# A gather queue on GpSimd: every second gather of one table waits for the landing of that table's gather before last

## The chip, the core and the metric

The kernel runs on one core of a Trainium2 chip. The metric is the time of one execution in microseconds on the device. A run is timed without the profiler; one further execution is profiled and gives the trace. Engines: TensorE (PE; its weight loads are PEld), VectorE (DVE), ScalarE (ACT), GpSimd (POOL), and SyncE (SP), which here issues the loads of the weights. Transfers are done by 16 DMA engines, whichever engine issues them.

## The reference, cut to what matters

Two transformer blocks run one after the other over 256 tokens of width 1024 in float32. The first ends in a product-key expert layer, which is the stage of the change:

```
idx = 16 experts of 16384 for each of 8 heads          # 128 experts for each token
u   = take(u_tab, idx)                                  # [tokens, 128, 1024]
a   = einsum('chkd,cd->chk', u, x)                      # a dot product for each token and expert
wgt = g * gelu(a)
v   = take(v_tab, idx)
out = einsum('chk,chkd->cd', wgt, v)                    # weighted sum of 128 rows for each token
```

Ahead of it are the modulation, attention and a short convolution; behind it the whole second block (a state space mixer, a linear attention in chunks, a feed-forward of width 4096).

## The kernel before, in words

The 256 tokens are two tiles of 128 tokens, one token on each partition. Each tile has 128 experts, so the stage has 256 steps, e = 0 to 255, here called experts (EXPERTS = 128 for a tile). For each e one row of each table is fetched for each of the 128 tokens:

- **u(e)**, the gather of the first table (`peer_u`, line 687): 128 rows of 4 KB into one of NU = 5 buffers of the tensor `gathered`. Its landing raises the semaphore `u_full[e % 5]` by 16.
- **v(e)**, the gather of the second table (`peer_v`, line 701): as many bytes into one of NV = 7 buffers. Its landing raises `v_full[e % 7]` by 16.

GpSimd issues both kinds from one program, in the order u(0), v(0), u(1), u(2), v(1), u(3), v(2), u(4), v(3) and so on: v(e) stands behind u(e+1). It has nothing else to do in the stage. Since an engine works off its program in order, a wait ahead of one gather holds all gathers behind it. All gathers go through one queue of transfers.

The consumers follow the landings. VectorE multiplies u(e) with the tile's tokens and adds up (`dot_expert`, line 2489), then raises `dot_ready` by 1. ScalarE takes the dot through the gelu, multiplies it with the gate and writes it on a diagonal, `diag[e % 8]` (lines 1737 to 1746). TensorE multiplies this diagonal with v(e) in two matmuls of 512 columns (`sum_expert`, line 1143; the trace shows two records for each matmul and each weight load, four for an expert) and accumulates in PSUM; after every odd e it raises `pair_summed` by 1. Between the experts TensorE does other products, by tables such as WQ_AT, and VectorE the routing of later heads; SyncE loads weights of 2 MB each when a buffer for them comes free.

What keeps a gather from overwriting rows in use are waits on GpSimd: u(e) waits for `dot_ready` to reach e - 4, and v(e) for `pair_summed` to reach `pairs(e - 6)`, which is (e - 5) // 2. The sum of expert e - 7, whose buffer v(e) takes, is then done.

Of the kernel before, what the change touches and what calls it, by code (L numbers as in the profile page):

```python
# [70 lines left out]
NV = 7  # L71
# [173 lines left out]
def pairs(experts):  # L245

    return (experts + 1) // 2


def build(nc, T, out):  # L250

    with ExitStack() as ctx:
# [3 lines left out]
        def sem(name):  # L256
            return ctx.enter_context(nc.semaphore(name))
# [187 lines left out]
        v_full = [sem(f"v_full{i}") for i in range(NV)]  # L445
        S_ = {}

        def flag(name):

            if name not in S_:  # L450
                S_[name] = sem(name)
            return S_[name]

        def group_wait(eng, name, i):
            g = (name, i)
            eng.wait_ge(bank_full[GROUP_BANK[g]], GROUP_USE[g] + 1)
# [52 lines left out]
        def turn_wait(eng, *u):  # L509

            eng.wait_ge(turned, turn_no[u] + 1)
# [124 lines left out]
        def _(pool):  # L636
# [55 lines left out]
            def gather_v(e):  # L692

                r, k, slot = e // ROUTE, e % ROUTE, e % NV
                if e >= NV:
                    pool.wait_ge(flag("pair_summed"), pairs(e - NV + 1))
                if e == 0:
                    turn_wait(pool, "m", 1, 0)
                if e == 3:
                    group_wait(pool, "out1", 1)  # L700
                pool.indirect_dma_start(  # L701
                    v_rows[:, slot, :], None, T["peer_v"],
                    bass.IndirectOffsetOnAxis(ap=expert_idx[:, r % 2, k:k + 1], axis=0),
                ).then_inc(v_full[slot], 16)

            gather_u(0)
            gather_v(0)
            gather_u(1)
            for e in range(1, TT * EXPERTS):
                if e + 1 < TT * EXPERTS:  # L710
                    gather_u(e + 1)
                gather_v(e)
# [2468 lines left out]
```

## Time and profile before

| | us |
|---|---|
| timed, median of 3 (lowest to highest) | 1310.25 (1309.9 to 1311.06) |
| span of the profiled execution | 1366.9 |
| of it ahead of the gathers | 150 |
| of it the stage of the gathers | 762 |
| of it behind them | 455 |

The profiled execution is 56.6 us longer than the median of the timed ones. Busy time is the sum of an engine's instructions. A row that ends in `<-` and a name says what ended the idle time ahead of an instruction; "issue" means that nothing which the profile shows did, "remote" that the semaphore moved but the profile can't name who moved it. The two gathers appear as DMA_INDIRECT on POOL; their duration there is that of the issue, not of the transfer.

### The profile page before, as it was taken

Reading aid. Unit: us, or ns where it says so; the run is one execution under the profiler, and the core shown is the slowest. Engines: PE = TensorE matmul, PEld = TensorE weight load, DVE = VectorE, ACT = ScalarE, POOL = GpSimd, SP = SyncE. Lnnn points to the kernel's source line nnn. Section 1 sums busy time; section 2 is a strip of 40 time slices with the busy share of each in tenths; the row PEclk is TensorE's granted clock in tenths of the full one; section 3 lists DMA queues with packets and bytes.
Section 4 is the critical chain, followed back from the end, with each engine's and each line's share of the span. In section 5 each row is a group of like instructions: output and inputs, shape, how many; then the busy total and the mean of one; then the engine's idle time right before and its main releaser. Section 6 shows DMA issues by size and latency. Waiting matters only on the chain. (4 is left out here: it accounts for less than half of the span.)

```text
span 1366.9 us, 14592 instructions
## 1 busy us (share of the span) xinstructions
PE 1199.9 (88%) x4663; PEld 665.4 (49%) x4663; DVE 861.8 (63%) x1765; ACT 420.2 (31%) x1138; POOL 500.2 (37%) x580
## 2 busy tenths in 40 slices
PE   7899888888778978876788889789999999999997
PEld 4676554433344542222345433236544545999443
DVE  2657669574663654776746557679989543676345
ACT  2213334344223343343423324432323311222000
POOL 1000356666665666766666666630000000000000
PEclk9999999999998999999999999999999999999999
DMA  9998789999998999999999999986644444454450
GB/s 358 390 349 326 286 319 339 367 357 367 364 366 300 406 403 405 407 377 364 340 371 353 400 405 409 377 306 233 224 139 148 145 150 156 157 175 145 175 184 31
DMA packets 134303, 405.66 MB, mean 297 GB/s; under 512 B 10153, under 2 KB 11585, under 8 KB 133971
## 3 DMA queue, kind: packets, MB, share of 16 engines
q0 software_dynamic: 75024, 273.19, 53.1%
q1 hardware_dynamic: 57860, 127.48, 25.8%
q10 hardware_dynamic: 1342, 4.06, 0.8%
q8 instruction: 38, 0.62, 0.2%
q14 instruction: 39, 0.31, 0.1%
HBM read 403.12 MB, written 1.05 MB: 296 GB/s over the span
## 5 line engine op out<-in xcount | busy, mean ns | idle before, releaser
L1143 PE MATMUL psum<-gathered,modr 128*128 128x512 f32 x1024 | 505.0, 633 | 130.3 <-DMA gathered<-in_peer_v_dram,expert_idx 49.0
L2489 DVE CUSTOM_DVE_ANT_0 gathered<-gathered,psum 128x1024 f32<-128x1024 f32 x256 | 311.5, 1217 | 202.3 <-DMA gathered<-in_peer_u_dram,expert_idx 153.3
L1143 PEld LDWEIGHTS psum<-gathered,modr 128*128 128x128 f32 x1024 | 190.7, 199 | 404.7 <-issue 284.9
L687 POOL DMA_INDIRECT gathered<-in_peer_u_dram,expert_idx x256 | 244.9, 957 | 240.5 <-DVE expert_idx L1997 144.0
L701 POOL DMA_INDIRECT gathered<-in_peer_v_dram,expert_idx x256 | 242.6, 947 | 169.9 <-remote 73.7
L780 PE MATMUL psum<-featT,weight_ring 128*128 128x128 f32 (+2 forms) x960 | 145.3, 305 | 14.4 <-issue 11.3
L780 PEld LDWEIGHTS psum<-featT,weight_ring 128*128 128x128 f32 x960 | 133.7, 196 | 43.9 <-issue 35.6
L780 PE MATMUL psum<-weight_ring,featT 128*128 128x512 f32 x336 | 147.9, 596 | 1.3 <-ACT featT L1563 0.8
L1737 ACT ACTIVATE gel<-dots 128x1 f32<-128x1 f32 x256 | 51.1, 200 | 255.1 <-issue 128.1
L1746 ACT ACTIVATE modr<-ident,wgt 128x128 f32<-128x128 f32 x256 | 102.8, 402 | 18.5 <-issue 1.1
L780 PEld LDWEIGHTS psum<-weight_ring,featT 128*128 128x128 f32 x336 | 62.6, 190 | 78.8 <-issue 76.6
L1741 ACT ACTIVATE wgt<-gel,expert_gate 128x1 f32<-128x1 f32 x256 | 75.4, 294 | 17.9 <-issue 0.3
L1989 DVE TENSOR_TENSOR work<-work 128x1088 f32<-128x1088 f32 (+5 forms) x87 | 68.6, 801 | 9.6 <-issue 2.8
L725 POOL DMA_DIRECT2D gathered<-in_b_in_dram x6 | 5.3, 942 | 138.6 <-ACT gathered L1585 104.2
L1585 ACT COPY work<-psum 128x128 f32<-128x128 f32 x32 | 8.4, 262 | 81.5 <-remote 44.6
L1978 ACT ACTIVATE work<-work,pack 128x256 f32<-128x256 f32 x28 | 12.7, 500 | 56.8 <-DVE work L1989 56.8
L1989 DVE TENSOR_TENSOR vectors<-weight_ring 128x1024 f32<-128x1024 f32 x14 | 16.5, 1220 | 20.9 <-PE psum L1512 20.9
L1563 ACT COPY featT<-psum 128x512 f32<-128x512 f32 (+1 forms) x24 | 12.4, 554 | 55.0 <-PE psum L752 53.8
L780 PE MATMUL psum<-weight_ring,uT 128*128 128x512 f32 x64 | 28.2, 593 | 1.0 <-ACT gathered L1585 1.0
L1989 DVE TENSOR_TENSOR gathered<-gathered,psum 128x256 f32<-128x256 f32 (+1 forms) x17 | 8.6, 511 | 29.8 <-PE psum L780 24.9
L1473 PE MATMUL psum<-featT,weight_ring 128*128 128x128 f32 x224 | 27.3, 275 | 0.0
L1473 PEld LDWEIGHTS psum<-featT,weight_ring 128*128 128x128 f32 x224 | 26.1, 192 | 0.0
(443 smaller groups left out, 1343.1 us busy)
## 6 DMA issues: line engine op xcount, KB each, us to landing
weight_ring<-in_w_in_dram SPq DMA_DIRECT2D x16, 2048.0 KB
weight_ring<-in_w_up_dram SPq DMA_DIRECT2D x8, 2048.0 KB
weight_ring<-in_w_down_dram SPq DMA_DIRECT2D x8, 2048.0 KB
weight_ring<-in_ada_w_dram SPq DMA_DIRECT2D x5, 2048.0 KB
work<-in_ada_w_dram SPq DMA_DIRECT2D x5, 2048.0 KB, 16.3
weight_ring<-in_peer_wq_dram SPq DMA_DIRECT2D x3, 2048.0 KB
gathered<-in_ada_w_dram SPq DMA_DIRECT2D x2, 2048.0 KB, 14.5
gathered<-in_peer_u_dram,expert_idx POOLq DMA_INDIRECT x256
```

The source lines that it names most:

```text
L687: pool.indirect_dma_start(u_rows[:, slot, :], None, T["peer_u"], bass.IndirectOffsetOnAxis(ap=expert_idx[:, r % 2, k:k + 1], axis=0),).the ...
L701: pool.indirect_dma_start(v_rows[:, slot, :], None, T["peer_v"], bass.IndirectOffsetOnAxis(ap=expert_idx[:, r % 2, k:k + 1], axis=0),).the ...
L780: last = pe.matmul(psum[0:m, bank, 0:n], lhs(k), rhs(k), start=(k == 0), stop=(k == kt - 1))
L1143: mm = pe.matmul(psum[:, SUM_BANK + half, :], diag[:, e % 8, :], v_rows[:, slot, 512 * half:512 * (half + 1)], start=(e % EXPERTS == 0), s ...
L1473: last = pe.matmul(psum[:, UP_BANKS * (n % 2) + bank, at:at + P], a(g, m), b(g), start=(g == 0), stop=(g == 3))
L1563: ins = act.activation(dst, src, func, **kw) if func else act.copy(dst, src)
L1737: act.activation(gel[:, col:col + 1], dots[:, col:col + 1], ACT.Gelu_apprx_tanh)
L1741: act.activation(wgt[:, col:col + 1], gel[:, col:col + 1], ACT.Copy, scale=expert_gate[:, r % 2, k:k + 1])
L1746: act.activation(diag[:, e % 8, :], ident[:, :], ACT.Copy, scale=wgt[:, col:col + 1]).then_inc(flag("diag_full"), 1)
L1978: act.activation(ffT[:, k, :], ffT[:, k, :], ACT.Relu, bias=pk("b_up")[:, k:k + 1])
L1989: return dve.tensor_tensor(o, a, b, op)
L2489: dve.tensor_tensor_reduce(u_rows[:, slot, :], u_rows[:, slot, :], h2_rows[t], 1.0, 0.0, ALU.mult, ALU.add, dots[:, col:col + 1])
```

## The change

From e = 8 on, an even v(e) no longer waits for `pair_summed`. It waits until v(e-2) has landed: for `v_full[(e - 2) % 7]` to have been raised by all gathers into that buffer up to v(e-2). Odd v(e) and all u(e) are unchanged.

```
             def gather_v(e):
 
                 r, k, slot = e // ROUTE, e % ROUTE, e % NV
-                if e >= NV:
+                if e >= NV and e % 2:
                     pool.wait_ge(flag("pair_summed"), pairs(e - NV + 1))
+                elif e >= NV:
+                    pool.wait_ge(v_full[(e - 2) % NV], 16 * ((e - 2) // NV + 1))
                 if e == 0:
                     turn_wait(pool, "m", 1, 0)
```

The order in which GpSimd's instructions stand is the same; what each waits for is not. This is GpSimd's program before, from v(8) on (v(8), u(10), v(9), u(11), v(10), u(12)); the name in brackets is the semaphore:

```order
L701 DMA gathered<-in_peer_v_dram,expert_idx 128x1024 [waits pair_summed]
L687 DMA gathered<-in_peer_u_dram,expert_idx 128x1024 [waits dot_ready]
L701 DMA gathered<-in_peer_v_dram,expert_idx 128x1024 [waits pair_summed]
L687 DMA gathered<-in_peer_u_dram,expert_idx 128x1024 [waits dot_ready]
L701 DMA gathered<-in_peer_v_dram,expert_idx 128x1024 [waits pair_summed]
L687 DMA gathered<-in_peer_u_dram,expert_idx 128x1024 [waits dot_ready]
```

And this is the same place of the changed program, where the gathers of the second table have moved to line 703:

```order
L703 DMA gathered<-in_peer_v_dram,expert_idx 128x1024 [waits v_full6]
L687 DMA gathered<-in_peer_u_dram,expert_idx 128x1024 [waits dot_ready]
L703 DMA gathered<-in_peer_v_dram,expert_idx 128x1024 [waits pair_summed]
L687 DMA gathered<-in_peer_u_dram,expert_idx 128x1024 [waits dot_ready]
L703 DMA gathered<-in_peer_v_dram,expert_idx 128x1024 [waits v_full1]
L687 DMA gathered<-in_peer_u_dram,expert_idx 128x1024 [waits dot_ready]
```

v(8) now waits for buffer 6, into which v(6) went, and v(10) for buffer 1, into which v(8) went. Three gathers stand between the one that is waited for and the one that waits.

## Rows read from the trace of the kernel before

**Rows 1.** The page: the span and the slices of it.

```profile
span 1366.9 us, 14592 instructions
...
GB/s 358 390 349 326 286 319 339 367 357 367 364 366 300 406 403 405 407 377 364 340 371 353 400 405 409 377 306 233 224 139 148 145 150 156 157 175 145 175 184 31
```

**Rows 2.** Busy time by window: the gathers' stage.

```profile
core 0: us, PE busy (x) PEld busy (x) DVE busy (x) ACT busy (x) POOL busy (x), PEclk, DMA share, GB/s
150.00:912.00 762.00, 619.97 (x1851) 298.83 (x1851) 480.80 (x1164) 283.48 (x881) 487.42 (x512) 0.95 0.97 371
```

**Rows 3.** Busy time by window: single stretches of the stage.

```profile
286.00:299.00 13.00, 10.77 (x36) 5.01 (x34) 8.09 (x16) 6.39 (x15) 9.91 (x11) 1.00 0.99 389
205.00:240.00 35.00, 29.01 (x96) 15.04 (x95) 31.04 (x92) 14.17 (x42) 23.78 (x25) 0.90 0.95 339
349.00:361.00 12.00, 8.13 (x28) 3.75 (x27) 8.56 (x29) 2.73 (x10) 8.75 (x10) 1.00 0.90 307
820.00:860.00 40.00, 36.65 (x83) 14.98 (x82) 28.86 (x69) 18.17 (x52) 27.11 (x29) 1.00 1.03 410
```

**Rows 4.** Busy time by window: the stage cut in five.

```profile
155.00:205.00 50.00, 43.28 (x149) 22.96 (x148) 32.92 (x98) 18.13 (x51) 29.87 (x32) 0.93 0.92 334
205.00:440.00 235.00, 190.93 (x617) 97.71 (x616) 146.97 (x361) 87.12 (x275) 150.59 (x159) 0.93 0.95 351
440.00:540.00 100.00, 82.70 (x287) 42.04 (x285) 55.07 (x129) 35.71 (x115) 64.27 (x67) 0.97 1.03 404
540.00:760.00 220.00, 173.96 (x455) 78.84 (x456) 144.85 (x355) 80.11 (x256) 143.70 (x152) 0.93 0.97 371
760.00:912.00 152.00, 124.10 (x314) 53.12 (x313) 97.07 (x202) 61.13 (x183) 96.83 (x102) 0.99 1.02 399
```

**Rows 5.** GpSimd in order of time: start, duration, engine, line, idle before.

```profile
349.51 0.94 POOL L701 DMA_INDIRECT gathered<-in_peer_v_dram,expert_idx  x1 [3.56 <-remote]
350.75 0.94 POOL L687 DMA_INDIRECT gathered<-in_peer_u_dram,expert_idx  x1 [0.30 <-issue]
```

**Rows 6.** GpSimd's waits in 150 to 912 us: total, times, longest.

```profile
POOL gathered L701 <- remote: 73.7, 29, 4.2
...
POOL gathered L701 <- PE psum L1143: 28.7, 12, 8.7
```

**Rows 7.** Line 701 up to 303.05 us, and line 1143 up to 294.8 us.

```profile
L701 POOL DMA_INDIRECT gathered<-in_peer_v_dram,expert_idx x50: 934/941/1451, 153.5 to 303.0; - x50
...
L1143 PE MATMUL psum<-gathered,modr x176: 592/592/1193, 167.6 to 292.7; 128*128 128x512 f32 x176
```

**Rows 8.** Line 687 up to 291.5 us, line 2489 up to 298 us.

```profile
L687 POOL DMA_INDIRECT gathered<-in_peer_u_dram,expert_idx x48: 934/938/1197, 152.0 to 291.0; - x48
...
L2489 DVE CUSTOM_DVE_ANT_0 gathered<-gathered,psum x48: 1199/1214/1222, 162.2 to 297.7; 128x1024 f32<-128x1024 f32 x48
```

**Rows 9.** Line 687 up to 232.5 us, line 2489 up to 238 us.

```profile
L687 POOL DMA_INDIRECT gathered<-in_peer_u_dram,expert_idx x27: 934/939/1197, 152.0 to 231.2; - x27
...
L2489 DVE CUSTOM_DVE_ANT_0 gathered<-gathered,psum x27: 1200/1212/1222, 162.2 to 237.5; 128x1024 f32<-128x1024 f32 x27
```

**Rows 10.** Line 701 up to 350 us, line 1143 up to 353.95 us.

```profile
L701 POOL DMA_INDIRECT gathered<-in_peer_v_dram,expert_idx x66: 934/941/1451, 153.5 to 349.5; - x66
...
L1143 PE MATMUL psum<-gathered,modr x261: 589/592/1193, 167.6 to 353.9; 128*128 128x512 f32 x131
```

**Rows 11.** Line 687 up to 487 us, line 2489 up to 503 us.

```profile
L687 POOL DMA_INDIRECT gathered<-in_peer_u_dram,expert_idx x113: 934/941/1413, 152.0 to 486.7; - x113
L2489 DVE CUSTOM_DVE_ANT_0 gathered<-gathered,psum x113: 1199/1220/1222, 162.2 to 502.8; 128x1024 f32<-128x1024 f32 x113
```

**Rows 12.** TensorE's weight loads in 155 to 912 us: what they wait for most.

```profile
PEld psum L1143 <- DMA gathered<-in_peer_v_dram,expert_idx: 115.4, 79, 3.2
```

**Rows 13.** Line 701 in 440 to 540 us and in 760 to 912 us.

```profile
L701 POOL DMA_INDIRECT gathered<-in_peer_v_dram,expert_idx x34: 934/941/942, 440.0 to 539.3; - x34
L701 POOL DMA_INDIRECT gathered<-in_peer_v_dram,expert_idx x52: 932/941/1147, 760.3 to 904.9; - x52
```

More of the change, by code:

```diff
@@ L694, in gather_v @@
                 r, k, slot = e // ROUTE, e % ROUTE, e % NV
-                if e >= NV:
+                if e >= NV and e % 2:
                     pool.wait_ge(flag("pair_summed"), pairs(e - NV + 1))
+                elif e >= NV:
+                    pool.wait_ge(v_full[(e - 2) % NV], 16 * ((e - 2) // NV + 1))
                 if e == 0:
```

## The prediction, made before the changed kernel was run

> **What bounds the kernel now.** Start with the page: the span of the profiled execution is 1366.9 us, and its line of GB/s stands between 286 and 409 for the first 27 of 40 slices and drops to about half when the expert stage is over [rows 1]. The stage of the gathers (150 to 912 us) is 762 us long and moves data at 371 GB/s; ahead of it and behind it lie 605 us, which the change does not touch [rows 1, 2]. So the second view is the same table cut finer, and the number to look for is the fastest rate that is held for long: 410 GB/s at 820 to 860 us [rows 3], and 404 over 440 to 540 us [rows 4]. One gather is 128 rows of 4 KB, 524,288 bytes; four gathers, the work of two experts, are 2.097 MB and take 5.12 us at 410 GB/s. The whole stage, 371 GB/s x 762 us = 283 MB, would take 690 us at that rate. No engine is that near its limit: in the cuts of the stage TensorE is busy 79 to 87%, VectorE 55 to 66%, and only the transfers reach their full rate for long [rows 4]. The transfers bound the stage, wherever they are kept fed.
>
> Who feeds them is GpSimd. An undisturbed issue is 0.94 us and the gap behind it 0.30 us [rows 5], so four gathers are issued in 4.98 us, against 5.12 us for their transfers. It leads by 0.14 us in four gathers, hence hardly at all. Its own waits are the third view: in the stage 73.7 us in 29 waits and 28.7 us in 12 waits of the line of the second table's gathers [rows 6]. What those 41 waits wait for is the pair of sums. One of them is odd: the 50th gather (expert 49) is issued at 303.0 us, and needs the sums of experts 42 and 43; their last of 176 TensorE records starts at 292.7 us [rows 7]. The count came ten microseconds later than the rows let expect. I can't explain it; it may belong to the profiled execution alone, which is 56.6 us longer than the median of the timed runs (1310.25 us). I come back to this below.
>
> **What the change does, part by part.** *The removed wait costs and hides nothing.* Gather e (even) asked for (e-5)//2 pairs of sums; gather e-1, just ahead of it on the same engine, asks for the same number: 10 and 9 both ask for 2. The odd gathers keep their wait, so every buffer stays protected and the removal is worth 0.
>
> *The added wait.* 124 gathers (e = 8 to 254, even) wait for the landing of v(e-2); I call such a wait a gate. Between the issue of v(e-2) and the moment GpSimd comes to v(e) stand three other issues, u(e), v(e-1) and u(e+1): 4 x 1.245 = 4.98 us. The wait costs what the landing signal takes beyond 4.98 us. The trace shows how long that is, by matching counts. At 389 GB/s the 48th gather of the first table is issued at 291.0 us and the 48th dot product, which the landing releases, starts at 297.7 us: 6.7 us [rows 3, 8]. At a moderate load (339 GB/s) the 27th goes from 231.2 us to 237.5 us: 6.3 us [rows 3, 9]. Just after GpSimd had paused for 3.56 us, the 66th gather of the second table goes from 349.5 us to 353.9 us, where TensorE's 261st record, the first of the 66th expert, starts: 4.4 us [rows 5, 10]. That is the least I find. With weights on the same engines the 113th goes from 486.7 us to 502.8 us: 16.1 us [rows 11].
>
> So with the queue as it is, each gate would hold GpSimd for 6.7 + 0.3 - 4.98 = 2.0 us; and a gate that holds shortens the queue, which shortens the signal. The cycle of two experts settles where signal + 0.30 us equals the time of four transfers. It can't be under 5.12 us (transfers at full rate) nor over 6.7 + 0.3 = 7.0 us. The question is how fast the transfers run with only three gathers in flight instead of four or more. The rows say: not at full rate. In the 12 us after the pause of 3.56 us, in which GpSimd issued again at its usual pace, they run at 307 GB/s, 6.83 us for four; at 205 to 240 us at 339 GB/s, 6.19 us [rows 3, 5]. These two contain pauses, a gate does not empty the queue as a pause does, so I take a value under them: **5.7 us**, 0.58 us over 5.12. This is an estimate, chosen between 5.12 and 6.19.
>
> What is queued behind the gate is everything GpSimd has: u(e+2), v(e+1), u(e+3). The dot products on VectorE wait for u, ScalarE for the dots, TensorE for v and the weights of ScalarE. All of them already wait for transfers (TensorE's line 1143 for the second table 115.4 us in 79 waits) [rows 12], so a later gather is later work on each.
>
> *How many gates count.* In 440 to 540 us and 760 to 912 us the rates are 404 and 399 GB/s [rows 4], and 34 and 52 of the second table's gathers lie there [rows 13], 43 gates. While weights share the engines a late gather only lets the weights go first, so those gates are free: but the weights take a part of these stretches only. I count 9 of the 43, and all 81 of the others: 90 gates x 0.58 us = 52 us. From this I take 5 us for gates that fall on a wait which GpSimd has anyway [rows 6]: **+47 us, 1357 us** in the timed runs.
>
> *Against the execution's own time.* Outside the two fast stretches the profiled execution needs 505 us for 170 of the second table's gathers, 5.94 us for each pair of experts, already over my 5.7 [rows 4, 13]. The 41 waits above make the difference, and where they stand the gates hide in part. If they are the profile's, the timed stage is 762 - 57 = 705 us, close to the 690 us of full rate, and the whole +47 us is due. If they are real, the 57 us lie elsewhere and the gates add less, which is the second rival. On the profiled span I therefore expect some 35 us: about 1402 us.
>
> **The rivals.** *The wait is met in time, no change, 1310 us (12%).* If the signal comes within 4.98 us of the issue, no gate holds. For it speaks the 4.4 us of the 66th gather, and that three gathers in flight are 3 x 1.28 = 3.8 us of work. It decides from a signal under about 5.1 us at full rate; against it, the signal matched in a stretch at 389 GB/s (286 to 299 us) took 6.7 us [rows 3, 8]. A rule points here: the Trainium skill, page "DMA: Bandwidth & Descriptors", section "Anatomy of one DMA — SWDGE (gpsimd) path", fits a gather at about 2.0 us plus bytes over 436 GB/s. By that the signal of 524,288 bytes would come after an estimated 3.2 us and no gate would ever hold; the trace does not agree: 4.4 us just after a pause, 6.3 and 6.7 us with a queue.
>
> *The gates hide in waits that exist, 1318 to 1335 us (17%).* If the timed runs have the late sums too, their cycles last near 5.94 us already, and each of the 41 waits for sums lets the queue run down, so that the gate behind it finds its signal there. Of the 81 gates 40 are left, at 0.2 to 0.6 us each: 8 to 25 us.
>
> *The queue starves, 1395 us and more (8%).* If three in flight run as after a pause, 6.19 us a cycle: 90 x 1.07 = 96 us, 1406 us.
>
> *Faster, 1300 us (8%).* Fewer gathers ahead of a weight transfer give it the engines sooner: the 113th gather's 16.1 us shows two queues that delay each other [rows 11]. If TensorE gets its weights earlier, it sums earlier and the pair waits (up to 102 us in all) shrink. It decides once TensorE waits for weights in the stage; what its sums wait for most there is the second table itself [rows 12], so I price it at 10 us, a tenth of those waits.
>
> **How the numbers follow.** My own case (C between 5.4 and 6.1 us, 1330 to 1392 us) has 55%, the others 17, 12, 8 and 8%. The range must leave out no more than two in ten: from 1309 us, the near edge of "no change", to 1388 us, leaving out the faster case, the starved one and a little of each neighbour. A measurement of this kernel can tell about 0.2% (2.6 us) from no change. Faster by more: 8%; within it: 12%; slower by more: 80%.
>
> **What the changed profile would show.** GpSimd's list of waits should have a new entry at the second table's line, released by the landing of the second table, of about 100 waits of 0.4 to 1.5 us; the issue gap before every second gather of that table grows from 0.30 us to about 1. The rate in quiet stretches should fall from 410 to about 370 GB/s, while the weight stretch stays near 400. The signal should shorten to 5.1 to 5.6 us. The 150 us ahead of the first gather and the 455 us from the last sum on must stay. I am wrong if quiet stretches still show 410 GB/s with gates that hold (the queue of three is enough), if the gates do not hold at all, or if the stage shortens by a loss of the long pair waits.

## The result, and the profile after

| | us |
|---|---|
| timed before, median of 4 runs | 1310.26 |
| timed after, median of 4 runs (lowest to highest) | 1402.07 (1400.78 to 1404.38) |
| ratio, with its 95% interval | 1.0693 (1.0678 to 1.0708) |
| span of the profiled execution after | 1401.1 |

The change costs 91.8 us, 0.74 us for each of its 124 gates. The forecast was 1357 us with a range up to 1388: the sign was right, the size half of what came, and the time lies outside the range. It ended next to the rival called "the queue starves" (1406 us, 8%). One execution of the experiments below, one of ten with a landing six places back, took 2709 us, for a reason that no trace shows; no ratio counts it.

The page of the changed kernel, to be held against [rows 1]:

```profile
span 1401.1 us, 14592 instructions
...
DMA  9999799999999999998999999994935524544440
GB/s 359 386 355 328 291 356 355 369 347 349 364 347 373 380 350 362 355 357 324 363 354 361 343 381 361 353 328 140 325 113 158 150 91 163 176 152 171 180 180 30
```

The 400s are gone. From the sixth slice to the end of the stage nearly every slice lies between 343 and 381 GB/s, while the row of digits above still shows 9: the digits don't tell a starved queue from a full one, the GB/s do. The stage by windows, as in [rows 4], and the 455 us behind it:

```profile
155.00:205.00 50.00, 47.71 (x180) 26.49 (x179) 40.64 (x133) 21.46 (x62) 33.51 (x36) 1.00 0.98 362
205.00:440.00 235.00, 185.78 (x596) 88.33 (x595) 142.76 (x328) 88.11 (x273) 149.03 (x157) 0.99 0.97 357
440.00:540.00 100.00, 77.20 (x276) 40.15 (x275) 51.66 (x126) 34.13 (x107) 57.47 (x60) 0.98 0.98 365
540.00:760.00 220.00, 164.85 (x428) 68.55 (x427) 139.57 (x330) 78.88 (x244) 142.27 (x149) 0.98 0.96 353
760.00:912.00 152.00, 117.89 (x303) 50.44 (x301) 86.39 (x200) 53.50 (x161) 90.24 (x95) 0.97 0.97 360
...
946.00:1401.00 455.00, 444.41 (x2096) 270.42 (x2094) 298.74 (x428) 95.97 (x179) 7.00 (x9) 1.00 0.46 156
```

The rate is the same everywhere, 353 to 365 GB/s, in the stretches with weights too (before: 404 and 399 in the third and the fifth). GpSimd's waits in 150 to 945 us, which answer to [rows 6]:

```profile
POOL gathered L703 <- DMA gathered<-in_peer_v_dram,expert_idx: 146.9, 112, 4.5
POOL gathered L687 <- DVE expert_idx L1999: 144.4, 2, 143.8
POOL gathered L687 <- issue: 75.3, 247, 0.3
POOL gathered L703 <- issue: 58.7, 139, 7.3
```

112 waits for the landing of the second table, 1.3 us each in the mean. (The second row is the wait for the routing, ahead of the stage.) The long waits for sums, 73.7 and 28.7 us in [rows 6], are not there. TensorE waits where it did [rows 12], for longer: 317.2 us. The 115.4 us of [rows 12] are not the measure for it, since they come from an execution with late sums. In a second profile of the kernel before (`e10_before_again`, below) they are 224.1 us, so this wait grew 1.4 times. First the changed kernel, then that second profile:

```profile
PEld psum L1145 <- DMA gathered<-in_peer_v_dram,expert_idx: 317.2, 191, 5.5
```

```profile
PEld psum L1143 <- DMA gathered<-in_peer_v_dram,expert_idx: 224.1, 182, 3.4
```

One warning on the numbers before. The profiled execution that the prediction had was 56.6 us over the timed runs; the one after is not (1401.1 against 1402.07). So the two spans differ by 34.2 us while the timed runs differ by 91.8. The comparisons below are with a second profile of the kernel before, `e10_before_again`.

### The profile page after: what moved, and what is told of

It is laid out like the page before. It is cut to its first block, busy times and chain, and to the rows that moved or that the text cites. A ratio compares the mean times of both kernels' runs of the same rounds, so it can differ in the third digit from the quotient of the medians.

```text
span 1401.1 us, 14592 instructions
## 1 busy us (share of the span) xinstructions
PE 1198.8 (86%) x4663; PEld 651.9 (47%) x4663; DVE 867.5 (62%) x1765; ACT 425.4 (30%) x1138; POOL 506.9 (36%) x580
## 4 chain that ended last, share of the span: by engine, by line
DMA 49%; PE 32%; DVE 8%; issue 4%; POOL 3%; DVEq 2%; ACT 1%; ACTq 0%; SPq 0%; POOLq 0%
DMA gathered<-in_peer_v_dram,expert_idx 45%; PE psum L782 13%; PE psum L1475 6%; PE psum L1514 6%; DMA gathered<-in_peer_u_dram,expert_idx 3%; DVE work L1991 3%; POOL gathered L703 2%; POOL gathered L687 1%; DMA weight_ring<-in_ada_w_dram 1%; PE psum L902 1%; PE psum L805 1%; PE psum L875 1%; DVE gathered L1999 1%; DVE gathered L1991 1%; DVE work L2781 1%
## 5 line engine op out<-in xcount | busy, mean ns | idle before, releaser
L1145 PEld LDWEIGHTS psum<-gathered,modr 128*128 128x128 f32 x1024 | 181.0, 194 | 467.5 <-DMA gathered<-in_peer_v_dram,expert_idx 317.2
L703 POOL DMA_INDIRECT gathered<-in_peer_v_dram,expert_idx x256 | 250.1, 977 | 211.9 <-DMA gathered<-in_peer_v_dram,expert_idx 146.9
L782 PE MATMUL psum<-featT,weight_ring 128*128 128x128 f32 (+2 forms) x960 | 140.6, 302 | 3.0 <-DVE modr L1991 2.2
L1514 PE MATMUL psum<-weight_ring,work 128*128 128x512 f32 x56 | 25.3, 592 | 0.0
```

Source lines behind the costliest of these rows:

```text
L703: pool.indirect_dma_start(v_rows[:, slot, :], None, T["peer_v"], bass.IndirectOffsetOnAxis(ap=expert_idx[:, r % 2, k:k + 1], axis=0),).the ...
L782: last = pe.matmul(psum[0:m, bank, 0:n], lhs(k), rhs(k), start=(k == 0), stop=(k == kt - 1))
L1145: mm = pe.matmul(psum[:, SUM_BANK + half, :], diag[:, e % 8, :], v_rows[:, slot, 512 * half:512 * (half + 1)], start=(e % EXPERTS == 0), s ...
L1514: last = pe.matmul(psum[:, PRODUCT_BANK[i], :], a(g), b(g), start=(n == 0 and g == 0), stop=(n == WINOGRAD - 1 and g == 1))
```

## The experiments

All edits are to `gather_v`, in the two places of this form; the changed kernel is the base unless the text says otherwise. Times are given as the median and as the difference from the kernel before on the same chip (1311.9 to 1312.3 us there).

```
                if e >= NV and e % 2:
                    pool.wait_ge(flag("pair_summed"), pairs(e - NV + 1))
                elif e >= NV:                                            # which gates
                    pool.wait_ge(v_full[(e - 2) % NV], 16 * ((e - 2) // NV + 1))   # on which landing
```

**The removed wait alone** (`e1_removed_only`): the last two lines are gone.

```
-                elif e >= NV:
-                    pool.wait_ge(v_full[(e - 2) % NV], 16 * ((e - 2) // NV + 1))
```

> The wait for the pair of sums is taken from the even gathers of the second table and nothing is put in its place. The order and every other wait stay. My theory: the odd gather just ahead asks for the same count, so the removed wait is worth 0 and the whole +92 us is the added wait's: 1310 us, within 0.3%. Rival: GpSimd's even waits also keep it from running ahead at a bad moment, and taking them away costs part of the 92 us: then 1320 us or more.

1311.89 us, ratio 1.0001 (0.9991 to 1.0010). The removal alone is worth nothing, as predicted; the whole cost comes with the added wait.

**The kernel before, profiled again** (`e10_before_again`, no edit).

> The kernel before itself, profiled once more. If the late sums of its first profile (73.7 us in 29 waits of GpSimd, a span 56.6 us over the timed runs) belong to that one execution: a span of about 1309 us, 406 GB/s at 205 to 425 us and hardly a wait for sums. If any profile of this kernel has them: a span near 1367 us again, with waits of some 100 us in all.

One timed run, 1311.88 us; span 1310.2 us. GpSimd's waits in 150 to 860 us and the window 205 to 425 us:

```profile
POOL gathered L687 <- DVEq L2491: 79.0, 114, 2.4
POOL gathered L701 <- issue: 74.2, 242, 0.5
POOL gathered L687 <- issue: 42.7, 140, 0.3
POOL gathered L718 <- PE psum L1143: 12.5, 1, 12.5
POOL gathered L701 <- PE psum L1143: 5.2, 14, 1.2
...
205.00:425.00 220.00, 194.35 (x672) 98.08 (x671) 152.80 (x367) 93.80 (x293) 160.99 (x171) 1.00 1.02 406
```

The gathers' waits for sums are 5.2 us in 14 waits, not 102 us in 41. The late sums belonged to that one execution. What holds GpSimd here are the buffers of the first table: the first row says that u(e) waited 114 times, 79.0 us in all, for a dot product to free its buffer. Less the gap of 0.30 us that stands ahead of every issue anyway, this is some 45 us. So GpSimd gets as far ahead as the buffers let it, at least at these 114 places. The kernel before runs its quiet stretches at 406 GB/s, where its first profile has 351 and 371 [rows 4]: the 5.12 us a cycle that the prediction took for the timed runs were nearly the right base (5.15 us at 407 GB/s).

**How far back the landing lies** (`e2_landing_four_back`, `e7_five_apart`, `e8_six_apart`, `e11_three_apart`). The gates stay, 124 of them; what they wait for changes. In the order of the queue v(e-4) lies eight places back, v(e-3) six, u(e-1) five, v(e-2) four, u(e) three.

```
-                    pool.wait_ge(v_full[(e - 2) % NV], 16 * ((e - 2) // NV + 1))
+                    pool.wait_ge(v_full[(e - 4) % NV], 16 * ((e - 4) // NV + 1))   # e2
+                    pool.wait_ge(v_full[(e - 3) % NV], 16 * ((e - 3) // NV + 1))   # e8
+                    pool.wait_ge(u_full[(e - 1) % NU], 16 * ((e - 1) // NU + 1))   # e7
+                    pool.wait_ge(u_full[e % NU], 16 * (e // NU + 1))               # e11
```

> Even gathers of the second table wait for the landing of v(e-4) instead of v(e-2): seven issues stand between instead of three, 8 x 1.245 = 10.0 us. My theory (the cost is what the landing signal takes beyond the issues between): the signal of 5.4 to 6.7 us is long there, so 1310 us, at most 5 us more from the weight stretches, where a signal took 16.1 us before. Rival (a wait on GpSimd for a transfer's semaphore costs by itself, whenever it is met, for example as a slow instruction): 124 times the same 0.74 us, 1402 us.

> Even gathers of the second table wait for the landing of v(e-3), six places back. Six places are 7.7 us. My theory: 1310 us, at most 6 us more, although GpSimd will be seen waiting for landings (with six in flight a landing took 7.7 to 8.9 us after the issue). Rival (the rate needs six in flight): 1320 to 1340 us.

> Even gathers of the second table wait for the landing of u(e-1), the gather just ahead of v(e-2) in the queue: five places back instead of four. My theory: a gate starves the transfers by what landing (5.6 us with a short queue) plus 0.55 us until the next issue exceed the places between; five places are 5 x 1.28 = 6.4 us at full rate against 6.15 us, so at most 0.1 to 0.2 us a gate where a landing is late: 1310 to 1330 us. Rival (a queue shorter than the usual six loses rate, by how short it is): about half of the loss of four places, 1345 to 1365 us.

> Even gathers of the second table wait for the landing of u(e), three places back instead of four. With the least landing seen (4.9 us after a held issue, 0.26 us until the next) a cycle of four gathers cannot be under 4.9 + 0.26 + 1.25 = 6.4 us, and four places gave 5.9 to 6.2 us, a us over their own floor of 5.2: here 6.4 to 7.3 us, so 1435 to 1525 us, my value 1480 us. Rival (the loss grows evenly with the places taken, +11 us for five and +92 us for four): 1484 us and more, so the run does not tell these two apart well; it gives the curve.

| places back | us | ratio (95%) | against before, us | GB/s at 205 to 425 us |
|---|---|---|---|---|
| 8 | 1311.72 | 0.9998 (0.9988 to 1.0007) | 0 | 406 |
| 6 | 1312.33 | 0.9998 (0.9988 to 1.0008) | 0 | 405 |
| 5 | 1323.45 | 1.0086 (1.0069 to 1.0103) | +11 | 399 |
| 4, the change | 1402.07 | 1.0693 (1.0678 to 1.0708) | +92 | 356 |
| 3 | 1546.96 | 1.1802 (1.1780 to 1.1823) | +235 | 296 |

GpSimd's waits for landings at 205 to 425 us, of the kernels with eight, six, five and three places; then the same row of the changed kernel, which has four:

```profile
POOL gathered L703 <- DMA gathered<-in_peer_v_dram,expert_idx: 6.0, 3, 3.1
```

```profile
POOL gathered L703 <- DMA gathered<-in_peer_v_dram,expert_idx: 13.6, 17, 3.5
```

```profile
POOL gathered L703 <- DMA gathered<-in_peer_u_dram,expert_idx: 19.5, 25, 3.4
```

```profile
POOL gathered L703 <- DMA gathered<-in_peer_u_dram,expert_idx: 74.6, 31, 2.9
```

```profile
POOL gathered L703 <- DMA gathered<-in_peer_v_dram,expert_idx: 43.2, 36, 3.4
```

Six places: GpSimd waits 17 times for a landing in this stretch and it costs nothing that the runs can tell, so neither the wait instruction nor a held GpSimd is the price; the kernel before is held too, by its buffers. Five places cost 11 us, the fifth place taken away costs 81 us more, and the fourth another 143. For three places I had the cycle right (6.4 to 7.3 us; 2.097 MB at 296 GB/s are 7.08 us) and turned it into too low a time (1435 to 1525 us): 124 x (7.08 - 5.15) is +239 us, where 5.15 us is the cycle at the 407 GB/s of the kernel before.

What changes with the places is also how long a gather is under way. These are the issues of transfers at 205 to 425 us: count, and median us from issue to landing. The kernel before (second profile), then five places back, then the changed kernel:

```profile
gathered<-in_peer_u_dram,expert_idx POOLq DMA_INDIRECT x86, 8.2
gathered<-in_peer_v_dram,expert_idx POOLq DMA_INDIRECT x85, 8.3
```

```profile
gathered<-in_peer_u_dram,expert_idx POOLq DMA_INDIRECT x82, 6.2
gathered<-in_peer_v_dram,expert_idx POOLq DMA_INDIRECT x81, 6.2
```

```profile
gathered<-in_peer_u_dram,expert_idx POOLq DMA_INDIRECT x75, 6.0
gathered<-in_peer_v_dram,expert_idx POOLq DMA_INDIRECT x75, 5.9
```

With the queue cut to five places the transfers keep nearly their full rate and a landing takes 6.2 us. Cut to four they lose 12%, and the landing comes hardly sooner, 6.0 us; cut to three they lose 27%, with medians of 5.9 and 5.6 us. So with five places, 6.4 us of transfers at 1.28 us each, the queue is just long enough for a landing of 6.2 us; with four, 5.1 us, it is shorter than the landing takes, and the rate falls. The runs show these numbers, not why a landing in a short queue takes 6 us.

**Where the gates stand** (`e3_quiet_gates`, `e4_weight_gates`): the 81 outside the stretches with weights, and the 43 in and near them.

```
-                elif e >= NV:
+                elif e >= NV and not (96 <= e < 130 or e >= 204):        # e3
+                elif e >= NV and (96 <= e < 130 or e >= 204):            # e4
```

> The new wait stands only at the 81 even gathers outside the weight stretches (not at experts 96 to 129 nor from 204 on); the 43 others have no wait of their own. If all 124 gates cost alike, 92 / 124 = 0.74 us each: +60 us, 1370 us. If the gates under weights are free, as the prediction nearly had it (9 of 43 count), the 81 others carry the whole: 1395 to 1402 us, 1.1 us each. If the weight stretches are dearer, since GpSimd was seen to be held 3 to 5.8 us by single gates there: 1345 to 1360 us.

> The counterpart: the new wait stands only at the 43 even gathers of experts 96 to 129 and from 204 on, in or near the weight stretches. All gates alike: 43 x 0.74 = +32 us, 1342 us. Gates under weights free: 1310 to 1317 us. Weight stretches dearer: 1350 to 1365 us.

e3: 1371.08 us, ratio 1.0464 (1.0440 to 1.0488), +59.2 us or 0.73 us a gate. e4: 1339.46 us, ratio 1.0211 (1.0190 to 1.0232), +27.6 us or 0.64 us a gate. Together 86.8 of the 91.8 us. The gates in and near the weight stretches are together nearly as dear as the others. The transfers in 400 to 520 us, in which the first three loads of weights lie in both, say why: first the kernel before (second profile), then the changed one. q0 is the queue of the gathers, q1 that of the weights:

```profile
DMA packets 14728, 48.56 MB, mean 405 GB/s; under 512 B 1352, under 2 KB 1352, under 8 KB 14720
...
q0 software_dynamic: 11420, 41.58, 87.4%
q1 hardware_dynamic: 3300, 6.89, 15.3%
```

```profile
DMA packets 13422, 43.79 MB, mean 365 GB/s; under 512 B 1208, under 2 KB 1208, under 8 KB 13416
...
q0 software_dynamic: 10116, 36.83, 82.3%
q1 hardware_dynamic: 3300, 6.89, 15.6%
```

Weights are 6.9 of 48.6 MB, a seventh of what moves there. The 4.75 MB that the changed kernel moves less there are gathers: a fixed amount of weights can't fill what held gathers leave for 120 us. While many weights do move, they fill it. The changed kernel cut finer, in turn with many and with few of them (q1 moves 1.50, 0.64, 3.53 and 0.02 MB in these four windows):

```profile
433.00:448.00 15.00, 11.93 (x49) 7.32 (x48) 6.59 (x18) 3.94 (x14) 7.39 (x9) 0.89 1.04 406
448.00:466.00 18.00, 15.27 (x64) 8.48 (x62) 13.42 (x43) 6.03 (x22) 10.89 (x12) 1.00 0.94 336
466.00:490.00 24.00, 16.11 (x65) 9.57 (x66) 9.31 (x25) 4.94 (x18) 10.34 (x11) 0.93 1.03 400
490.00:505.00 15.00, 12.97 (x52) 7.12 (x51) 9.60 (x15) 7.73 (x21) 9.55 (x10) 1.00 0.94 347
```

Gates hold GpSimd for 4.50 us up to 441.42 us and for 4.21 us up to 486.51 us, inside the first and third window, and the transfers stay at 406 and 400 GB/s. In the other two windows they run at 336 and 347. No run has gates only under moving weights, so their price by themselves is not measured.

**How many gates** (`e5_every_fourth`, `e12_every_eighth`, `e9_every_sixteenth`, `e6_every_gather`).

```
-                elif e >= NV:
+                elif e >= NV and e % 4 == 0:       # e5; e % 8 in e12, e % 16 in e9
```

In `e6_every_gather` the gate stands at every v(e) from e = 7 on (249 gates), behind the odd ones' wait for the sums:

```
-                elif e >= NV:
+                if e >= NV:
```

> The new wait stands only at every fourth gather of the second table (e = 8, 12, ... 252), 62 of the 124; the other even ones have no wait. If a gate costs by itself what it lets the queue run down, 62 x 0.74 = +46 us, 1358 us. Rival: the queue rebuilds between gates, and the loss comes only of a gate that meets a queue still short from the gate before: 1320 to 1335 us.

> Every gather of the second table from e = 8 on waits for the landing of v(e-2), twice the gates; the odd ones keep the wait for the sums too. My theory (what counts is the time of landing plus wake-up over four gathers, so that the two chains of gates run beside each other with the same cycle): 1402 us, at most 10 us more. Rival (a cost for each gate): 248 x 0.74 = +184 us, 1495 us.

> The new wait stands only at e = 16, 32, ... 240, 15 gates with 32 gathers between. Theory A (new, from the run with every fourth: at 205 to 425 us it moved 357 GB/s, as little as the changed kernel's 356 with twice the gates): one gate leaves the queue short, a short queue runs at 1.47 us a gather instead of 1.28, and GpSimd, which issues in 1.245 us, wins back only 0.23 us of lead a gather. It takes some 10 to 15 gathers to be back at the full rate, 2 to 3 us lost for each gate: 15 x 2.5 = +37 us, 1350 us (1340 to 1357). Theory B (the price measured with every fourth, 79 / 62 = 1.27 us, is that of any single gate): +19 us, 1331 us. Theory C (a full queue of six covers one gate): 1312 us.

> The new wait at e = 8, 16, ... 248, 31 gates with 16 gathers between. Theory A: the queue has just about recovered when the next gate comes, 31 x 2.2 = +68 us, 1380 us (1365 to 1388). Theory B: 31 x 1.27 = +39 us, 1351 us. Theory C: 1312 to 1320 us.

| gates | us | ratio (95%) | against before, us | us a gate |
|---|---|---|---|---|
| 15 (every 16th) | 1333.95 | 1.0172 (1.0151 to 1.0192) | +21.8 | 1.45 |
| 31 (every 8th) | 1354.08 | 1.0329 (1.0296 to 1.0361) | +41.9 | 1.35 |
| 62 (every 4th) | 1391.48 | 1.0605 (1.0579 to 1.0630) | +79.2 | 1.27 |
| 124, the change | 1402.07 | 1.0693 (1.0678 to 1.0708) | +91.8 | 0.74 |
| 249 (every one) | 1438.14 | 1.0967 (1.0944 to 1.0990) | +125.8 | 0.51 |

This was the surprise. A lone gate is not worth 0.74 us but nearly twice that, and with half the gates most of the cost stays. Each of the two theories I had for the run with every fourth missed (1358, and 1320 to 1335 us), and so did both for every gather (1402 to 1412, and 1495 us). For every eighth and sixteenth the constant price (theory B: 1351 and 1331 us) came within some 3 us; theory A had a recovery, which the trace shows, but its +68 and +37 us are 1.6 and 1.7 times what came.

One lone gate in the trace of `e9_every_sixteenth`. First GpSimd, then the transfers of 318 to 358 us in 40 slices of 1 us:

```profile
323.66 0.93 POOL L703 DMA_INDIRECT gathered<-in_peer_v_dram,expert_idx  x1 [0.30 <-issue]
324.89 0.94 POOL L687 DMA_INDIRECT gathered<-in_peer_u_dram,expert_idx  x1 [0.30 <-issue]
328.97 0.93 POOL L703 DMA_INDIRECT gathered<-in_peer_v_dram,expert_idx  x1 [3.13 <-DMA gathered<-in_peer_v_dram,expert_idx]
330.21 0.94 POOL L687 DMA_INDIRECT gathered<-in_peer_u_dram,expert_idx  x1 [0.30 <-issue]
331.45 0.93 POOL L703 DMA_INDIRECT gathered<-in_peer_v_dram,expert_idx  x1 [0.30 <-issue]
```

```profile
DMA  9999999999998798999989999999999999999999
GB/s 410 406 406 418 401 410 410 418 406 406 410 397 234 254 320 303 340 397 299 332 320 401 401 381 422 410 414 422 406 426 401 434 410 414 389 414 401 401 422 418
```

GpSimd stands still for 3.13 us in place of 0.30. The transfers notice next to nothing until 330 us, one microsecond after it has begun to issue again. Then nine slices lie at 234 to 397 GB/s, and from 339 us they are back at 381 to 434, mostly over 400. The nine sum to 2799 KB where 9 x 410 are 3690: 891 KB, 2.2 us of work lost at this gate (1.45 us in the mean of the 15, by the timed runs). The hold is not the price. All 15 holds of this run:

```profile
POOL gathered L703 <- DMA gathered<-in_peer_v_dram,expert_idx: 69.4, 15, 11.5
```

They are 4.6 us long in the mean and cost 1.45: most of a hold is paid out of the queue that stood ahead, and only the part in which the transfers run short is lost. The recovery takes 9 us, while GpSimd issues a gather each 1.24 us, hence seven. With a gate every fourth expert one comes each eight gathers, just as the queue is filled again; with the change one comes each four, in the midst of the recovery. In the trace of `e5_every_fourth` the rate falls to 246 GB/s behind the gate at 317.63 us and is back at 426 GB/s in the slice before the next, at 329.33 us. I take this for the reason why the second half of the gates adds only 12 us; the traces agree with it, and no run tests it alone.

## Why the prediction was right in sign and wrong in size

**"The removed wait costs and hides nothing"**: right (e1, 1.0001).

**"The added wait": a gate costs the signal beyond 4.98 us.** Right in kind: eight and six places cost nothing, five +11, four +92, three +235 us. Not in amount: the hold itself is not what the time pays (lone gates hold 4.6 us in the mean and cost 1.45), and the landing beyond which it is counted was longer in the kernel before than the 6.7 us matched in its first profile (medians of 8.2 us at 205 to 425 us and 11.2 at 540 to 760, in the second). The prediction did not price a gate by its hold, though, but by the rate of the short queue, which is what the runs show. GpSimd's list has the predicted row, with 112 waits where I said about 100, of 1.3 us each (I said 0.4 to 1.5).

**"The cycle of two experts settles" at 5.7 us: the smaller of the two failed terms.** At 357 GB/s in the quiet stretches it is 2.097 MB / 357 = 5.87 us against 5.15 us before, 0.73 us a gate (e3), not 0.58: 12 us on the 81 gates. I chose 5.7 between 5.12 and 6.19 with the argument that a gate does not empty the queue as a pause does. The runs show that the rate falls as far behind a gate: a lone gate costs 1.3 to 1.5 us, and the transfers behind the one shown run at 311 GB/s for nine microseconds (2799 KB), as those behind the pause did (307 GB/s) [rows 3]. The step that led there was that a gate "shortens the queue, which shortens the signal", to 5.1 to 5.6 us. The median only fell to 6.0 us. Two cycles of the changed kernel, each from one gate to the next:

```profile
395.31 0.94 POOL L703 DMA_INDIRECT gathered<-in_peer_v_dram,expert_idx  x1 [1.92 <-DMA gathered<-in_peer_v_dram,expert_idx]
...
400.50 0.93 POOL L703 DMA_INDIRECT gathered<-in_peer_v_dram,expert_idx  x1 [0.52 <-DMA gathered<-in_peer_v_dram,expert_idx]
...
408.07 0.94 POOL L703 DMA_INDIRECT gathered<-in_peer_v_dram,expert_idx  x1 [2.90 <-DMA gathered<-in_peer_v_dram,expert_idx]
```

5.19 us, then 7.57 us. The gather issued at 395.31 us, right behind a hold, let the next gate open at 400.50; the one issued then, after a hold of only 0.52 us, took until 408.07. That the second ran into the reduced rate is my reading. These two are long ones: the mean cycle of the stretch is the 5.87 us above.

**"How many gates count": 9 of the 43 in the fast stretches: the larger failed term.** They cost 27.6 us (e4), not 5, as if 38 of them counted at 0.73 us: 22 us too little. I reasoned that weights take the engines in the meantime, which holds while they move (406 and 400 GB/s, the windows above), and counted the share by eye, which was far off. The rows for it were there: 34 of the second table's gathers in 440 to 540 us [rows 13], and as many of the first are 68 x 0.524 = 35.7 MB, of the 40.4 MB that 404 GB/s move in 100 us [rows 4]. More than four fifths of the "weight stretch" were gathers. I said the rate would stay near 400 there; it fell to 365 and 360. One of these two errors alone would have stayed inside the range: 90 gates at 0.73 us give 1371 us, 124 at 0.58 give 1377, each with the 5 us taken off.

**"minus 5 us for gates that fall on a wait"**: nothing left of it. The waits that were to absorb them were those of one profiled execution. By terms: 81 gates +59 (I had 47), 43 gates +28 (I had 5), absorbed 0 (I had 5); 5 us more come when all stand together. That makes the 45 us between +47 and +92.

**"Against the execution's own time"**: half right. I suspected that the 57 us of late sums were the profile's, and e10 shows it. The span was forecast at about 1402 us and came to 1401.1, which is two errors that cancel: I expected the late sums in it again, with +35 us on top; they are gone, and the change costs 92.

**The rivals.** "Met in time" is refuted (112 waits). The Trainium skill, page "DMA: Bandwidth & Descriptors", section "Anatomy of one DMA — SWDGE (gpsimd) path", fits a DMA at about 2.0 us plus bytes over 436 GB/s, an estimated 3.2 us for a gather. The traces don't agree: at 205 to 425 us the medians are 5.6 to 8.6 us over the runs that have them, and the least of the second table in the changed kernel is 4.2 us. "The gates hide in waits" rested on the late sums, which timed runs don't have. "Faster" had no part: 0 us in e1, and with the gates only in and near the weights (e4) the time rises. "The queue starves" named what happened, a queue that runs as after a pause; it had 90 gates at 1.07 us for 96, where the runs have 124 at 0.74 for 92. I gave it 8% since I held its one row, 339 GB/s at 205 to 240 us, for a stretch with pauses; its rate was lower than what came (357) and its count too.

**Ahead and behind**: the first gather of the second table is issued at 153.4 us (153.5 before) and the 455 us behind the stage stand as before. The stage alone grew.

**A rule of thumb that would have given it**, worked out afterwards and only fitted: a gate costs the landing time at which the rate is still full (6.2 us, five places) plus the 0.30 us between issues [rows 5], less the places x 1.28 us. Four places: 6.5 - 5.1 = 1.4 us (1.27 to 1.45 measured, with gates four or more experts apart). Five: 6.5 - 6.4 = 0.1 us (11 / 124 = 0.09, but with a gate every second expert). Six: below nothing (0). Lone gates five or three places back were not run.

**What stays open** is why the transfers, with three and then four gathers issued and not landed, run below their rate, at 234 to 397 GB/s, for nine microseconds. In 375 to 384 us, behind another gate of e9, the engines' share is 0.93 at 341 GB/s, and 1.02 at 408 right after:

```profile
375.00:384.00 9.00, 8.08 (x37) 4.69 (x36) 5.54 (x9) 2.98 (x9) 6.92 (x7) 1.00 0.93 341
384.00:396.00 12.00, 10.36 (x34) 5.04 (x35) 5.57 (x12) 4.71 (x17) 9.20 (x10) 1.00 1.02 408
```

Of the 16% in rate 9% is share and the rest is a longer time for each byte. No run took these two apart. No variant beat the kernel before, and nothing here points to one: the quiet stretches already run at 406 and 407 GB/s.

## What to carry to other kernels

When a wait is added to the engine that feeds a queue of transfers, don't ask whether the transfer engines look busy. Ask how much work is issued ahead at the moment the wait opens, and compare it with the landing time at full rate: one place of 1.28 us more or less was the difference between +11 and +92 us. Work that the transfers miss where they are the limit is not won back, so holds of 4.6 us in the mean, one every 16 experts, already cost 1.7%. That a faster feeder than this one (1.245 us against 1.28) would fill the queue sooner is likely, but no run varied it. Before a stretch is called free because something else shares the engines, count its bytes by queue.

## What the runs showed of the hardware that I had not expected

- A profiled execution can carry waits that the timed ones don't have: of two profiles of the same kernel one spans 1366.9 us with 102 us of waits for sums, the other 1310.2 us with 5.2.
- The time from issue to landing grows with the queue and buys 1.5% of rate from five places to six and nothing beyond: medians of 6.2 us at 399 GB/s, 7.3 us at 405, 8.2 us at 406.
- After one hold of 3.13 us the transfers ran below their rate for 9 us, beginning a microsecond after the issues had resumed.
- With weights moving on a second queue the transfers held 400 and 406 GB/s through holds of more than 4 us; where few or none moved they ran at 336 and 347.
